# Expert mixing by 8 tokens and 16 slots, with four column groups on TensorE

## The reference, cut to what matters

```
v1, i1 = top_k(s1, 16); v2, i2 = top_k(s2, 16)      # scores against 128 + 128 keys
sv, si = top_k(v1[:, None] + v2[None, :], 16)       # 16 best sums of 256
expert = e1 * 128 + e2                              # 16 of 16384 experts
g = softmax(sv)
act = gelu(einsum('phkd,pd->phk', u[expert], x))    # 1024-long dot with the token
out = einsum('phk,phkd->pd', g * act, v[expert])    # weighted sum over all 8*16 rows
```

## Time and profile before

| | |
|---|---|
| time, median of 3 runs | 3308.49 us (3305.99 to 3310.06) |
| span of the profiled execution | 3302.0 us |
| mixing stage within it, first weight to last mix | 597.0 to 3294.0 us |
| busy: PE / DVE / ACT / POOL | 87% / 67% / 65% / 42% |
| read from HBM | 1179 MB, of which gathers are 1056 x 1.05 MB |

### The profile page before, as it was taken

The page is one execution under the profiler, slowest core; times in us unless marked ns, Lnnn a source line. Parts: engine busy times, 40 slices in busy tenths (PEclk is TensorE's granted clock), DMA queues, the critical chain, the costliest instruction groups (busy, mean ns, idle before and its releaser), DMA issues. The chain is left out here.

```text
span 3302.0 us, 33384 instructions
## 1 busy us (share of the span) xinstructions
PE 2886.4 (87%) x9454; PEld 1408.2 (43%) x9454; DVE 2218.7 (67%) x5274; ACT 2154.6 (65%) x7216; POOL 1392.2 (42%) x1135
## 2 busy tenths in 40 slices
PE   7999999888888888888898888888988898889886
PEld 5665455444434433444344344343443344434321
DVE  5687265776676667666766676667666766676665
ACT  3332143677777777777777777777777777777775
POOL 0000110455544555554455544544555445544553
PEclk9999999999999999999999999999999999999999
DMA  7232133999999999999999999999999999999997
GB/s 284 87 104 76 30 122 125 369 419 418 420 419 403 419 420 420 414 420 420 420 396 420 420 420 419 420 421 418 403 420 420 420 413 420 420 418 406 421 420 302
DMA packets 170079, 1190.91 MB, mean 361 GB/s; under 512 B 20058, under 2 KB 21498, under 8 KB 30242
## 3 DMA queue, kind: packets, MB, share of 16 engines
q0 software_dynamic: 155808, 1118.53, 82.1%
q1 hardware_dynamic: 14084, 70.23, 5.7%
HBM read 1179.42 MB, written 9.25 MB: 360 GB/s over the span
## 5 line engine op out<-in xcount | busy, mean ns | idle before, releaser
L929 PE MATMUL ps<-r_w,r_yT 128*128 128x512 f32 (+1 forms) x2712 | 1320.6, 622 | 256.2 <-ACT r_yT L1255 253.4
L604 POOL DMA_INDIRECT r_w<-in_peer_uv,gidx x678 | 860.5, 1269 | 880.3 <-PE ps L929 841.8
L1806 DVE SCALAR_TENSOR_TENSOR r_w<-r_w,r_qk 128x1024 f32<-128x1024 f32 x678 | 829.9, 1225 | 499.9 <-DMA r_w<-in_peer_uv,gidx 494.7
L929 PEld LDWEIGHTS ps<-r_w,r_yT 128*128 128x128 f32 (+1 forms) x2712 | 485.8, 192 | 1018.3 <-ACT r_yT L1255 600.8
L929 PE MATMUL ps<-r_yT 128*128 128x512 f32 (+1 forms) x904 | 443.7, 620 | 72.4 <-ACT r_yT L1255 70.1
L1247 ACT ACTIVATE mixc<-mixc 128x1 f32<-128x1 f32 x1056 | 207.8, 197 | 449.5 <-DVE r_w L1806 286.0
L1255 ACT ACTIVATE r_yT<-ident,mixc 128x128 f32<-128x128 f32 x1024 | 411.3, 402 | 33.2
L1252 ACT ACTIVATE mixc<-mixc 128x1 f32<-128x1 f32 x1056 | 408.9, 387 | 35.0
L1251 ACT ACTIVATE mixc<-mixc 128x1 f32<-128x1 f32 x1056 | 408.7, 387 | 33.8
L604 POOL DMA_INDIRECT r_yT<-in_peer_uv,gidx x226 | 298.5, 1321 | 269.4 <-PE ps L929 257.3
L1806 DVE SCALAR_TENSOR_TENSOR r_yT<-r_yT,r_qk 128x1024 f32<-128x1024 f32 x226 | 276.6, 1225 | 176.1 <-DMA r_yT<-in_peer_uv,gidx 175.9
(11 more groups left out here) (293 smaller groups left out, 2777.3 us busy)
## 6 DMA issues: line engine op xcount, KB each, us to landing
r_w<-in_ada_w SPq DMA_DIRECT2D x18, 1024.0 KB, 5.3
r_w<-in_peer_uv,gidx POOLq DMA_INDIRECT x678
r_w<-in_w_lin SPq DMA_DIRECT2D x16, 512.0 KB, 6.9
r_vo<-in_x_prompt SPq DMA_DIRECT2D x8, 512.0 KB, 7.2
r_qk<-in_ada_w SPq DMA_DIRECT2D x2, 2048.0 KB, 16.7
r_w<-in_w_out SPq DMA_DIRECT2D x2, 2048.0 KB, 8.9
r_w<-in_x_prompt SPq DMA_DIRECT2D x8, 512.0 KB, 3.5
x_dram<-r_w POOLq DMA_DIRECT2D x8, 512.0 KB, 3.4
```

Source lines behind the costliest of these rows:

```text
L604: pool.indirect_dma_start(ring[i], None, table, bass.IndirectOffsetOnAxis(gidx_t[:, h, j:j + 1], 0)).then_inc(e_ld[i], 16)
L929: mm = nc.tensor.matmul(ps[0:r, 2 * p + c, :], diag[:, j % 4, 0:r], row[:, D + c * 512:D + (c + 1) * 512], start=h == 0 and j == 0, stop=h ...
L1806: V.scalar_tensor_tensor(ring[i][:, 0:D], ring[i][:, 0:D], 1.0, h2[:, t, :], ALU.mult, ALU.mult, accum_out=dots[:, i:i + 1]).then_inc(dot_ ...
```

## The change

A slot is now 8 tokens by the 16 experts of one head: group `g` of 16 groups, partition `16*j + s` holding expert `s` of token `8*g + j`. There are as many slots as before (128 a tile, 32 for the sample).

- Indices and gates. Before, a column of the index table was one expert number of 128 tokens. Now the table is turned: DVE spreads a head's 16 indices over a 128x128 matrix (`xi`), one matmul against `eg` turns them (`turn_places`), DVE copies them to `gidx` (`copy_places`). The gates go the same way (`xg`, `turn_gates`, `copy_gates` on ACT).
- Token rows. Each of the 8 tokens is needed on 16 partitions. PE makes this of 32 rows of `h2` with a matrix of zeros and ones (`replicate`, two matmuls of 512 columns), ACT copies the 128x1024 result out of PSUM into one of two buffers (`copy_rows`). One such build serves all slots of one group `g` in a set of heads. `SETS` gives the sets: one head at a time, then two, then four. Build `b+1` is made on PE ahead of the first mix of build `b`, and copied on ACT ahead of the first weight of build `b`.
- The weighted sum. The stationary matrix has 32 columns (the group's 8 tokens among 32), and the 1024 columns of `v` are taken in four matmuls of 256, each into its own 32 partitions of PSUM. A tile's sum now fills two banks, and all tiles use the same two.
- ACT's chain for a weight loses one copy; its last instruction writes 128x32 in place of 128x128.
- The routing is started at slots listed in `ROUTE_AT`; for some heads (`FAST`) it takes 11 slots, for the others 16.
- The sum of squares of the last normalization is added over four partition blocks by a small matmul (`sum_squares`). Loads and stores of a tile's residual and result are four DMAs each in place of one.
- The opening makes the new constants on DVE and drops one on POOL.

The diff, cut to its core:

```diff
-K_ROUTE, K_GATE, K_W, K_FIN = 13, 2, 3, 3
+K_ROUTE, K_W, K_FIN = 14, 3, 5
+GRP, NG = 8, 16
+QC = 256
+SETS = [((0,), (1,), (2, 3), (4, 5), (6, 7)), ((0, 1), (2, 3), (4, 5, 6, 7))] + [
+    ((0, 1, 2, 3), (4, 5, 6, 7))] * (NT - 3) + [((0,), (1,))]
+FAST = (2, 3, 12, 13, 14, 15)
+ROUTE_AT = {2: 2, 3: 10, 4: 22, 5: 37, 6: 53, 7: 69, 8: 85, 9: 101, 10: 116, 11: 132,
+            12: 146, 13: 154, 14: 162, 15: 170, 16: 180}
+ROUTE_AT.update({m: 180 + 16 * (m - 16) for m in range(17, (NT - 1) * HEADS + S_STEPS)})
...
+        slots, builds, first = [], [], []
+        for t in range(NT):
+            for heads_of in SETS[t]:
+                for g in range(NG if t < NT - 1 else GROUPS):
+                    builds.append((t, g))
+                    first.append(len(slots))
+                    for h in heads_of:
+                        for c in ([g] if t < NT - 1 else [GROUPS * i + g for i in range(GROUPS)]):
+                            slots.append((t, h, g, c, len(builds) - 1, number(t, heads_of[-1])))
...
+        def build_at(s):
+
+            return first.index(s) + 1 if s in first and first.index(s) + 1 < len(builds) else None
...
# SP
-                sp.dma_start(x1s[0:r], src).then_inc(x1_ld, 16)
+            def finish(t, nq, src, dst):
+                for c in range(4):
+                    sp.dma_start(x1s[c * DEC:(c + 1) * DEC, 0:nq, :],
+                                 src[:, c * QC:(c + 1) * QC].rearrange("(q j) n -> j q n", q=nq)).then_inc(x1_ld, 16)
                 sp.wait_ge(y_out, t + 1)
...
# POOL
+            for n, (t, h, g, c, b, m) in enumerate(slots):
+                i = place[n]
+                if n == 0 or m != slots[n - 1][5]:
+                    pool.wait_ge(idx_ready, m + 1)
+                if uses[n] > 1 or i < RING:
+                    pool.wait_ge(v_free, RING + last_use[n] + 1)
...
+                pool.indirect_dma_start(ring[i], None, table,
+                                        bass.IndirectOffsetOnAxis(gidx_t[:, t % 2, h, c:c + 1], 0)).then_inc(e_ld[i], 16)
...
# PE
+            def turn_places(m):
+
+                pe.wait_ge(idx_x, m + 1)
+                if m:
+                    pe.wait_ge(gate_ready, m)
+                nc.tensor.matmul(ps[:, 6, 16:32], xi.rearrange("p j s -> p (j s)"), eg, start=True, stop=True).then_inc(idx_t, 1)
...
+            def replicate(b):
+
+                t, g = builds[b]
+                if b:
+                    pe.wait_ge(x_copy, b)
+                q = slice(g // 4 * DEC, (g // 4 + 1) * DEC)
                 for c in range(2):
-                    mm = nc.tensor.matmul(ps[0:r, 2 * p + c, :], diag[:, j % 4, 0:r], row[:, D + c * 512:D + (c + 1) * 512],
-                                          start=h == 0 and j == 0, stop=h == steps(r) - 1 and j == TOPK - 1)
+                    mm = nc.tensor.matmul(ps[:, 2 + c, :], spread[q, (g % 4) * P:(g % 4 + 1) * P],
+                                          h2[q, t, c * 512:(c + 1) * 512], start=True, stop=True)
+                mm.then_inc(x_rep, 1)
+
+            def mix(s):
+
+                t, h, g, _, _, _ = slots[s]
+                pe.wait_ge(dg_ready, s + 1)
+                if t and s == t * TILE_SLOTS:
+                    pe.wait_ge(acc_free, t)
+                row, q = ring[place[s]], g // 4
+                new, end = s == spans[t, q // 2][0], s == spans[t, q // 2][-1]
+                for c in range(4):
+                    mm = nc.tensor.matmul(ps[c * DEC:(c + 1) * DEC, q // 2, (q % 2) * QC:(q % 2 + 1) * QC], diag[:, s % 4, :],
+                                          row[:, D + c * QC:D + (c + 1) * QC], start=new, stop=end)
                 mm.then_inc(v_free, 1)
...
+            for s in range(N_SLOTS):
+                t, j = slots[s][0], s - slots[s][0] * TILE_SLOTS
+                for m in routes(s):
+                    if s - ROUTE_AT[m] == 0 and m < number(NT - 1, 0):
+                        query(*tile_head(m), tile_head(m)[0] % 2)
+                b = build_at(s)
+                if b:
+                    replicate(b)
+                mix(s)
...
# ACT
                 act.wait_ge(dot_done, s + 1)
-                nc.scalar.activation(sq[:, i:i + 1], d, ACT.Square, scale=(TANH_K * GELU_C) ** 0.5)
-                act.wait_ge(v_free, s + 5)
-                nc.scalar.activation(kd[:, i:i + 1], d, ACT.Copy, scale=TANH_K)
-                wch.link(nc.scalar.activation(gd[:, i:i + 1], gate_t[:, h, j:j + 1], ACT.Copy, scale=d))
-                wch.link(nc.scalar.activation(th[:, i:i + 1], sq[:, i:i + 1], ACT.Tanh, scale=d, bias=kd[:, i:i + 1]))
+                wch.mark(nc.scalar.activation(sq[:, i:i + 1], d, ACT.Square, scale=GELU_C ** 0.5 / TANH_K))
+                nc.scalar.activation(gd[:, i:i + 1], gate_t[t % 2][:, h, c:c + 1], ACT.Copy, scale=d)
+                wch.need()
+                wch.link(nc.scalar.activation(th[:, i:i + 1], sq[:, i:i + 1], ACT.Tanh, scale=d, bias=d))
...
-                nc.scalar.activation(diag[:, j % 4, 0:r], (ident if r == P else sel32)[:, 0:r], ACT.Copy,
+                act.wait_ge(v_free, RING + s - 3)
+                lo = (NG // 4 - 1 - g % 4) * GRP
+                nc.scalar.activation(diag[:, s % 4, :], strip[:, lo:lo + DEC], ACT.Copy,
                                      scale=wc[:, i:i + 1]).then_inc(dg_ready, 1)
+            def copy_rows(b):
+
+                act.wait_ge(x_rep, b + 1)
+                if b >= 2:
+                    act.wait_ge(dot_done, first[b - 1])
+                nc.scalar.activation(xrep[b % 2], ps[:, 2:4, :].rearrange("p b n -> p (b n)"), ACT.Copy).then_inc(x_copy, 1)
...
+            for s in range(N_SLOTS):
+                t, j = slots[s][0], s - slots[s][0] * TILE_SLOTS
+                b = build_at(s)
+                if b:
+                    copy_rows(b)
+                weight(s)
...
# DVE
+            def dot(s):
+                i, b = place[s], slots[s][4]
+                if s == first[b]:
+                    dve.wait_ge(x_copy, b + 1)
                 dve.wait_ge(e_ld[i], 16 * uses[s])
-                V.scalar_tensor_tensor(ring[i][:, 0:D], ring[i][:, 0:D], 1.0, h2[:, t, :], ALU.mult, ALU.mult,
+                V.scalar_tensor_tensor(ring[i][:, 0:D], ring[i][:, 0:D], TANH_K, xrep[b % 2], ALU.mult, ALU.mult,
                                        accum_out=dots[:, i:i + 1]).then_inc(dot_done, 1)
```

More of the change, by code:

```diff
@@ L315, in build, with routes, tile_head, piece @@
             free.append((n, i))
[L317 to L327, removed]
+        slots, builds, first = [], [], []
[7 more added lines that the diff above has]
+                            slots.append((t, h, g, c, len(builds) - 1, number(t, heads_of[-1])))
+        assert len(slots) == N_SLOTS
+        first.append(N_SLOTS)
+        spans = {}
+        for n, x in enumerate(slots):
+            spans.setdefault((x[0], x[2] // 8), []).append(n)
+        N_ROUTES = number(NT - 1, S_STEPS)
+        def routes(s):
+            return [m for m in range(2, N_ROUTES) if 0 <= s - ROUTE_AT[m] <= 20]
+        def build_at(s):
+            return first.index(s) + 1 if s in first and first.index(s) + 1 < len(builds) else None
+        def tile_head(m):
+            return m // HEADS, m % HEADS
+        def piece(m):
+            return 10 if m in FAST else 15
         x_rows = [A["x_prompt"][0, t * P:(t + 1) * P, :] for t in range(NT - 1)] + [A["x_sample"][0]]
@@ L581, in _ @@
             table = A["peer_uv"]
[L583 to L605, removed]
@@ L920, in scores @@
                 for c in range(2):
-                    mm = nc.tensor.matmul(ps[:, 6, 0:1], qsq[:, c, :], ones[:, 0:1], start=c == 0, stop=c == 1)
+                    mm = nc.tensor.matmul(ps[:, 4, 384:385], qsq[:, c, :], ones[:, 0:1], start=c == 0, stop=c == 1)
                 mm.then_inc(r_mm, 1)
-            def mix(t, h, p, r, j):
-                pe.wait_ge(dg_ready, slot0(t, h) + (j + 1))
-                row = ring[place[slot0(t, h) + j]]
-                for c in range(2):
-                    mm = nc.tensor.matmul(ps[0:r, 2 * p + c, :], diag[:, j % 4, 0:r], row[:, D + c * 512:D + (c + 1) * 512],
-                                          start=h == 0 and j == 0, stop=h == steps(r) - 1 and j == TOPK - 1)
-                mm.then_inc(v_free, 1)
@@ L934, in _, with sum_squares @@
+            def sum_squares(t, nq):
+                pe.wait_ge(f_sq, t + 1)
+                for c in range(4):
+                    mm = nc.tensor.matmul(ps[c * DEC:(c + 1) * DEC, 7, 0:nq], sel32, fss[:, 0:nq], start=True, stop=True)
+                mm.then_inc(f_mm, 1)
+            pe.wait_ge(ld_nw, 32)
             pe.sem_inc(v_free, RING)
```

431 lines of the change are left out of this document (246 added, 185 removed).

## The result

The changed kernel takes 4626.5 us, median of four runs (4624.2 to 4641.9), beside 3309.3 (3306.0 to 3310.1) for the kernel before: a ratio of 1.400 [1.397, 1.402]. The forecast was 4080, the range 3560 to 4480: the direction was right, the size 546 us short, and the time lies outside the range.

What follows compares the result with a forecast made beforehand. The prediction took full DMA, 2.50 us a slot, as the bound before. Build, head, query and other terms made the stage 3259 us for 2697 (+562); with 209 for the clock, 4073 of span, 4080 forecast, range 3560 to 4480.

Steps and rivals of the forecast that it cites:

- The bound of before: Gather stage of the kernel before: DMA is full at 2.50 us a slot, and PE and the other engines have time to spare.
- The order and the stall: ACT's queue, each build: ACT stands still 2.57 us behind a mix and the replicate before copying, 1.0.
- The clock: PE in the gather stage: idling in every build brings stretches at 1.2 GHz; bounds 0 to 1045 us, taken as 209.
- the clock stays at half: PE, part of the much slower rival: 1.2 GHz throughout, 4915 us; chance 0.09 together with another mechanism.
- Head work: ACT, per head: two table loads and five small instructions no longer hidden, 4.0 us for each of 64 heads, 256 us.
- Weights: ACT's chain per slot: 1.65 us before, less 0.17 for a dropped instruction and a smaller diagonal, 1.48 us.
- Tile boundaries: A tile's first mix waits 1.2 us for DVE's product, but the replicate of 1.9 runs meanwhile: nothing.
- The start: Opening ahead of the first weight: some 2 us of DVE reductions beside other work, -1 to 3 us, taken as nothing.
- Full clock: Rival for the whole kernel: the forecast's sum with no clock term, 3870 us; chance 0.20.
- Only the first slots slow: Rival: only the first 192 slots lose time, later four-slot builds keep DMA's 10.0 us; 3580 us, chance 0.16.
- Not slower: Rival at each build's copy: a replicate of some 0.5 us leaves DMA the bound; 3260 us, chance 0.09.
- The column groups one behind another: PE's mix, part of the much slower rival (chance 0.09): groups run serially, 1.9 us for 0.57, +426 us on 4080.

Runs made afterwards that it cites:

- e8: The kernel before, with the second 512 columns of the weighted sum mixed only in each head's first and last slot: 3308.8 us, ratio 1.0002.
- e4: The changed kernel with only the first two builds made, all later replicates and copies left out: 3326.5 us, ratio 1.006 to the kernel before.
- e1: The changed kernel with filler matmuls put on idle PE in some 80% of the slots: 4182.3 us, ratio 1.265 to the kernel before.
- e3: The changed kernel with, in four-slot builds, the replicate behind the first mix and its copy ahead of the fourth weight: 3906.1 us, ratio 1.181.
- e6: The changed kernel with the routing of heads 17 and on started one slot later, query behind a build's first mix: 4620.3 us, ratio 1.397.

## Why the prediction was wrong

**The bound of before: right.** e8 shows it in the kernel before, and e4 agrees: with the grouped mixes and without the builds nothing is won.

**The order and the stall: right in mechanism.** The copy waits in each of 328 builds for the mix and the replicate ahead of it. Where the clock is at 2.4 GHz the stall is 2.64 (e1), for 2.57 forecast; the copy steps 0.92, for 1.0; a query adds 8.38 - 4.88 = 3.5, for 3.74. That 3.5 is a sum of two things: the query takes 5.38, since it begins at half clock, and gives 1.80 back, since the replicate behind it runs at full. Of the signs that the forecast named, the idle time ahead of every copy came; a mean clock of 0.8 to 0.9 did not.

**The clock: this is the step that failed.** The forecast put the term between 0 and 1045 us and took a fifth, 209. Measured, the stall of a bare build is 4.88 for 2.57 (164 of the 328 copies; most of the others wait longer, for head work or a query): 2.31 x 320 = 739 us, 530 more than taken. The argument was that about 3 us at half clock in 9.5, a third, would fall on mixes that hide under weights. It read the length of the slow stretch from the earlier trace rows, where mixes of 128 rows by 512 columns follow the idle time and the clock is back behind them. Here neither the mixes of four groups nor the replicates brought it back before the next idle time. The clock stayed down but for the stretches behind queries, and the share at half clock was nearly 0.9 (a mean of 0.56 out of 0.50 and 1.00) and not a third. Why this work does not bring it back stays open. The case "the clock stays at half" stood among the rivals at 4915 with, together with another mechanism, a chance of 0.09; it was the right mechanism. It lay 269 us above the profiled span: 255 because it doubled the queries too, and 51 because mix and replicate do not quite double (2.31 more, for 2.47), less 37 by the other errors below.

**Head work, 4.0 us a head: too small.** Sixteen slots take 55.20 us in the steady stretch (3000 us and on), four bare builds 4 x 11.21, a query 3.5: 6.86 remain, +183 us over 64 heads, if all are like these. By what is left, some 5 are ACT's, counted at 4.0. The other 1.9 the forecast left out: a head's scores stand on PE ahead of a mix and the replicate for which ACT waits, so that the copy's wait is 6.22 and the step from weight to weight 9.13, for 7.23:
```profile
3039.20 1.20 PE L954 MATMUL ps<-kTt,r_yT 128*128 128x128 f32 x4
3040.19 0.85 PE L956 MATMUL ps<-ones,r_yT 128*128 128x1 f32 x4
3040.97 1.08 PE L992 MATMUL ps<-r_w,r_yT 128*32 128x256 f32 x8
...
3041.98 3.78 PE L979 MATMUL ps<-r_qk,spread 32*128 32x512 f32 x4
...
3045.80 1.02 ACT L1355 ACTIVATE r_vo<-ps 128x1024 f32<-128x1024 f32 x1 [6.22 <-PE ps L979]
```

**Weights: too dear.** 1.33 us apart, for 1.48: -154 us over the 1024 slots that the sum priced this way, and -26 by the copies. The chain of the earlier trace rows held more than the two pieces that I took off. Against it, a build takes 11.22 where 4 x 1.33 + 0.92 + 4.88 make 11.12: the forecast let the stall begin with the next weight's step, 0.10 before the diagonal ends, +32 us. The queries give -14 and, with the sample's beside them, -12.

**Tile boundaries, "nothing": wrong by some 12 us.** The four builds behind a boundary take 61.2 to 61.6 us where four take 55.2, in each of the six tiles from the third on. But 4.0 of the 6.0 are the sample's query, which stands there and was counted: ACT's wait ahead of that copy is 12.42 us, for 8.38 behind an ordinary query. What is left is 2.0 us, six times; in the first two tiles it can't be told apart.

**The start, "at nothing": wrong by 12 us.** The first weight is at 609.42, for 597.00. The opening gives 3 of it (forecast -1 to 3). The rest is two replicates and two copies ahead of the first weight, the second replicate already at half clock:
```profile
604.69 3.77 PE L979 MATMUL ps<-r_qk,spread 32*128 32x512 f32 x4 [0.64 <-ACT r_yT L1355]
...
608.50 1.02 ACT L1355 ACTIVATE r_vo<-ps 128x1024 f32<-128x1024 f32 x1 [3.79 <-PE ps L979]
```

Together: 530 + 183 - 180 + 32 - 12 + 12 + 12 = +577 on the 4073 forecast for the span; the span is 4640.1, +567. 10 us are left over, in sizes that were not taken apart.

**The rivals.** Full clock (3870, 0.20): refuted by the PEclk row. Only the first slots slow (3580, 0.16): the late tiles take 13.9 us a build (2885 us for slots 192 to 1023), far over 10.0, but e3 is this case made true, with DMA full from tile 2 on and the early slots slow. Not slower (3260, 0.09): decided by a replicate of about 0.5 us, which took 3.78, and 1.98 at full clock; and e4 shows that even none at all does not reach it. The column groups one behind another: refuted by a step of 0.57 for eight records in e1, as in the earlier trace rows.

The forecast read the earlier trace rows wrongly where it says that a change of tiling mode does not show: the 0.57 there already holds one. Record by record, in e1 at 2.4 GHz, the second round of four grouped records starts 0.24 us behind the first and the replicate 0.33 behind the second; the replicate's second record comes 0.53 behind its first, its later ones 0.43 apart. From mix to query in the kernel before, where no mode changes, the next piece starts within 0.01 us of the pace inside a piece. So a change costs 0.2 us at 2.4 GHz, and 0.3 at 1.2 by the same reading. The Trainium skill's rule on tiling modes (TensorEngine Tiling, Key Properties), that a change of mode drains the array, agrees with these delays. They cost the sum nothing: the steps of 0.57 and 1.9 that it used contain them.

The range failed with the clock term. Its top, 4480, was set just short of the much slower case (4500 and up) on the strength of that case's chance of 0.09, although the working had no row of a ring with 2.5 us of idling in each turn and the bound of the unknown cost was the whole 1045.

## What to carry to other kernels

Where a change puts PE and another engine in turns on one path, price PE's work on it at 1.2 GHz first, and ask which piece of that work has been seen in a trace to bring the clock back. A step that waits for its neighbour in every turn belongs where other work lies between the two: here the copy went three weights later on ACT's queue, with the replicate one mix later on PE's, and that alone was worth 720 us, over half of the loss. When a wait is moved, look at what stands next on the waiting engine's queue (e6): the wait may only move along. And when a transfer is the bound, take the load off the busiest engine and look whether the time moves (e8) before building a scheme for it.

## What the runs showed of the hardware

- PE was busy 6.58 of 6.59 us on a grouped mix (128 rows by 32 columns), scores and a 32-row replicate, and stayed at 1.2 GHz; 5.4 us of 128x128 query work ended at 2.4 GHz. The forecast took it that work brings the clock back, as in the earlier trace rows. Over 400 us, e3 has 0.62 with PE busy for 343, the kernel before 0.98 with 350, and e8 0.85 with 282. The Trainium skill (TensorE: Matmul & The Clock Gate, Part 1) says that the gate goes by how busy the array has lately been; how this work counts there no row here shows.
- The same replicate reading 128 rows for 32 took as long by the record (3.77 and 3.78 at half clock), and the kernel took 101 us less, with the mean clock of a stretch at 0.66 for 0.56.
- More work made the kernel faster: with fillers PE has 1885 matmul records for 1380 in 400 us, and the kernel takes 444 us less.
- A mix of eight grouped records is stepped in 0.57 us at 2.4 GHz and 1.01 at 1.2; four records of 32 rows by 512 columns take 1.98 and 3.78.
- Where two neighbouring pieces of PE's work differ in tiling mode, the change delays PE by 0.2 us at 2.4 GHz and 0.3 at 1.2; each of the figures in the line above contains part of one.
